# Expert rows of tiles 2 and 3 gathered as one 8 KB row of u and v, v weighted by a diagonal matrix on TensorE

## The reference, cut to what matters

```python
s = einsum('nhpd,hpkd->nhpk', q, sub_keys)               # scores against two sets of 128 sub-keys
s_top, i_top = top_k(s, 16)                              # 16 best of each half
best, sel = top_k((s_top[..., 0, :, None] + s_top[..., 1, None, :]).reshape(n, 8, 256), 16)
expert, gate = ..., softmax(best)                        # 8 x 16 = 128 experts a token
a = einsum('nd,ned->ne', x, take(u, expert))             # a dot of the token with each u row
act = gelu(a) * gate
out = einsum('ne,ned->nd', act, take(v, expert))         # weighted sum of the v rows
```

## Time and profile before

| | |
|---|---|
| median of 3 runs | 1908.88 us (1908.41 to 1910.58) |
| the profiled execution | 1910.62 us, its span 1908.6 us |
| TensorE busy | 1289.2 us (68%), mean granted clock 0.797 |
| VectorE busy | 1155.7 us (61%) |
| ScalarE busy | 372.3 us (20%) |
| POOL busy | 1095.1 us (57%), 1152 gathers |
| DMA | 725.45 MB, 380 GB/s over the span; 604.05 MB of it the gathers |

### The profile page before, as it was taken

How to read it: one execution, slowest core, us unless ns; L and a number is a source line. 1 busy time by engine, 2 the same in 40 slices (tenths; PEclk the granted TensorE clock), 3 DMA queues, 4 the chain that set the end, 5 groups by cost and what they waited for, 6 DMA issues and landing times.

```text
span 1908.6 us, 20116 instructions
## 1 busy us (share of the span) xinstructions
PE 1289.2 (68%) x6613; PEld 757.4 (40%) x6613; DVE 1155.7 (61%) x3160; ACT 372.3 (20%) x947; POOL 1095.1 (57%) x1192
## 2 busy tenths in 40 slices
PE   7898689998777787899977766664543433333344
PEld 5777565657454555555645422221220100000010
DVE  3117965566377657767755774568766667666430
ACT  3321133441021123234311110111101001000000
POOL 0002455446466656565656557666777777777764
PEclk9899888999888889999999877777765566555666
DMA  8567989899999999999999999999999999999997
GB/s 318 174 224 262 395 334 369 315 382 410 397 411 410 412 410 409 374 410 409 385 412 411 411 406 405 399 410 398 409 409 409 410 408 406 406 408 402 404 373 301
DMA packets 187013, 725.45 MB, mean 380 GB/s; under 512 B 21888, under 2 KB 23168, under 8 KB 174240
## 3 DMA queue, kind: packets, MB, share of 16 engines
q0 software_dynamic: 165888, 604.05, 80.4%
q1 hardware_dynamic: 18624, 117.55, 15.8%
q10 hardware_dynamic: 2400, 2.58, 0.4%
HBM read 719.16 MB, written 5.00 MB: 379 GB/s over the span
## 4 chain that ended last, share of the span: by engine, by line
PE 32%; DMA 31%; DVE 14%; POOL 13%; issue 8%; ACT 2%; SPq 0%; ACTq 0%; POOLq 0%; DVEq 0%
DMA v_ring<-in_peer_v,idx_v 15%; DMA u_ring<-in_peer_u,idx_u 14%; PE summed L1052 8%; POOL v_ring L740 6%; POOL u_ring L723 6%; DVE u_ring L1638 6%; PE bank L801 5%; PE bank L919 4%; PE bank L865 3%; PE bank L908 2%; PE bank L878 2%; PE bank L870 1%; PE bank L1022 1%; PE bank L997 1%; PE bank L1000 1%
## 5 line engine op out<-in xcount | busy, mean ns | idle before, releaser
L1638 DVE SCALAR_TENSOR_TENSOR u_ring<-u_ring,h_psum 128x1024 f32<-128x1024 f32 x576 | 689.9, 1215 | 276.4 <-DMA u_ring<-in_peer_u,idx_u 262.9
L1052 PE MATMUL summed<-v_ring,spread 128*32 128x512 f32 x2240 | 445.6, 857 | 496.8 <-DMA v_ring<-in_peer_v,idx_v 496.6
L740 POOL DMA_INDIRECT v_ring<-in_peer_v,idx_v x560 | 528.8, 944 | 411.5 <-PE summed L1052 216.1
L723 POOL DMA_INDIRECT u_ring<-in_peer_u,idx_u x576 | 543.4, 943 | 214.0 <-issue 116.5
L1052 PEld LDWEIGHTS summed<-v_ring,spread 128*32 128x32 f32 x2240 | 92.5, 138 | 766.0 <-issue 762.0
L801 PE MATMUL bank<-w_ring,hT 128*128 128x256 f32 (+1 forms) x720 | 184.3, 415 | 8.3 <-DVE shared L1525 3.8
L801 PEld LDWEIGHTS bank<-w_ring,hT 128*128 128x128 f32 (+1 forms) x720 | 139.7, 199 | 46.8 <-issue 16.4
L919 PE MATMUL bank<-hT,w_ring 128*128 128x128 f32 (+2 forms) x768 | 137.3, 336 | 1.6 <-issue 0.8
L919 PEld LDWEIGHTS bank<-hT,w_ring 128*128 128x128 f32 x768 | 121.0, 195 | 29.5 <-issue 22.6
L865 PE MATMUL bank<-hT,w_ring 128*128 128x192 f32 (+1 forms) x512 | 107.1, 364 | 1.5 <-DVE shared L1432 1.5
L713 POOL CAST idx_u<-experts 128x16 uint32<-128x16 f32 x36 | 7.8, 216 | 164.5 <-DVE gates L1628 164.3
(11 more groups left out here) (209 smaller groups left out, 1404.3 us busy)
## 6 DMA issues: line engine op xcount, KB each, us to landing
w_ring<-in_w_proj SPq DMA_DIRECT2D x27, 1024.0 KB, 8.4
w_ring<-in_w_pq SPq DMA_DIRECT2D x24, 1152.0 KB, 8.9
w_ring<-in_w_gate SPq DMA_DIRECT2D x24, 1024.0 KB, 8.1
w_ring<-in_w_z SPq DMA_DIRECT2D x12, 1024.0 KB, 7.6
w_ring<-in_w_out SPq DMA_DIRECT2D x12, 1024.0 KB, 9.6
u_ring<-in_peer_u,idx_u POOLq DMA_INDIRECT x576, 8.9
v_ring<-in_peer_v,idx_v POOLq DMA_INDIRECT x560, 8.8
qx<-in_x_prompt SPq DMA_DIRECT2D x8, 512.0 KB, 8.7
```

The lines of the kernel that those rows point to most:

```text
L723: nc.gpsimd.indirect_dma_start(u_ring[:, i % RING, :], None, peer_u, bass.IndirectOffsetOnAxis(idx_u[:, g % 2, j:j + 1], 0)).then_inc(u_la ...
L740: nc.gpsimd.indirect_dma_start(ring[:, slot, :], None, peer_v, bass.IndirectOffsetOnAxis(idx_v[:, n % 2, j:j + 1], 0)).then_inc(landed[slo ...
L1052: mm = nc.tensor.matmul(summed[half][low:low + 32, :], spread[:, P * i + 32 * c:P * i + 32 * c + 32], rows[:, 512 * half:512 * half + 512] ...
L1638: nc.vector.scalar_tensor_tensor(u, u, 1.0, h_psum[:], ALU.mult, ALU.mult, accum_out=dots_sb[:, g % 2, j:j + 1]).then_inc(u_free, 1)
```

## The change

For tiles 2 and 3 (ticks 320 to 575, 256 gathers) a third table `peer_uv` holds the u and the v row of an expert side by side, 8 KB. One gather (`gather_row`) brings both for each of 128 tokens, 1 MB, into a slot of 8 KB a partition: the two rings are one tensor now, and 8 such slots cover it. The v gathers of tiles 0, 1 and 4 still run until tick 353, in what was `v_ring`; so the first 36 rows use only the 4 slots over `u_ring`.

The dot of a row is as before (`dot_row`). Then ScalarE works row by row: `spread_gate` writes the identity times the gates (128x128) into one of 8 buffers `diag`, two rows ahead; `weigh_row` applies gelu to the one column of dots and multiplies the diagonal with it. TensorE multiplies this diagonal matrix with the v half of the row (`row_sums`, two matmuls of 128x128 by 512 columns), accumulating in two PSUM banks: for tile 2 in banks 2 and 3, which the front work hands over (from tick 320 on its jobs use banks 0 and 1 only), for tile 3 in `summed`. A slot is free once TensorE is done with the row (`row_summed`). The turning of experts and of weights (`places_t`, `spread`, `weigh`) goes away for these tiles, and so do the 34 ticks of v gathers behind the last u gather. The head items of part C stand at ticks 1, 3, 5 and 7 of a group instead of 1 to 4, and the norms 10, 11 and 12 eight ticks apart.

```diff
+SPLIT = GROUPS_C * GROUP
+MERGED = GATHERS - SPLIT
+UNITS = GROUPS_C // 2
+TICKS = GATHERS + 6
+DIAGS = 8
+AHEAD = 2
+FEW = 36
...
+def slot_of_row(m):
+    return m % 4 if m < FEW else (4 + m - FEW) % 8
...
+            n, off = divmod(j - 1, 2 if part == "C" else 1)
+            if 2 <= h < HEADS and off == 0 and 0 <= n < len(head_items(part, h)):
+                here.append(head_items(part, h)[n])
+                if n < 2:
...
+        tick = tick_of_sum(units_of_tile(t)[-1], 7) + 1 if k < 3 else gathers_of_tile(t)[-1] + 2
+        at(tick).insert(0, ("collect", t))
+        if k == 2:
+            for n in range(3):
+                at(tick + 1 + 8 * n).insert(0, ("norm", 10 + n))
+        if k > 2:
+            at(tick + 1).insert(0, ("norm", 10 + k))
...
+            b = len(jobs) % (BANKS if len(jobs) < len(split_jobs) else 2)
+            jobs[job] = (b, jobs_in_bank[b])
+            jobs_in_bank[b] += 1
...
+        ring = sb("ring", [P, 2 * RING, D])
+        u_ring, v_ring = ring[:, 0:RING, :], ring[:, RING:2 * RING, :]
+        uv_ring = ring[:].rearrange("p (s r) d -> p s (r d)", r=2)
+        diag = hT_all[:, 1024:1024 + P * DIAGS].rearrange("p (i n) -> p i n", n=P)
...
+            def gather_row(m):
+                g, j = divmod(SPLIT + m, GROUP)
+                if j == 0:
+                    copy_indices(g)
+                slot, former = slot_of_row(m), former_row(m)
+                if former is not None:
+                    pool.wait_ge(row_summed, former + 1)
+                elif slot < 4:
+                    pool.wait_ge(u_free, SPLIT - RING + 2 * slot + 2)
+                else:
+                    pool.wait_ge(v_free, SPLIT // 4 - 1 + (slot - 4) // 2)
+                nc.gpsimd.indirect_dma_start(
+                    uv_ring[:, slot, :], None, peer_uv,
+                    bass.IndirectOffsetOnAxis(idx_u[:, g % 2, j:j + 1], 0)).then_inc(row_landed[slot], 16)
...
+            for tick in range(GATHERS):
+                if tick < SPLIT:
                     gather_u(tick)
-                if tick >= LEAD:
+                if LEAD <= tick < SPLIT + LEAD:
                     gather_v(tick - LEAD)
+                if tick >= SPLIT:
+                    gather_row(tick - SPLIT)
...
+            def row_sums(m):
+                t = group_place((SPLIT + m) // GROUP)[0]
+                mine = [i - SPLIT for i in gathers_of_tile(t)]
+                if m == mine[0] and t == 2:
+                    for b in (2, 3):
+                        pe.wait_ge(bank_used[b], jobs_in_bank[b])
+                elif m == mine[0]:
+                    pe.wait_ge(collected, 3)
+                pe.wait_ge(diag_ready, m + 1)
+                for half in range(2):
+                    mm = nc.tensor.matmul((bank[2 + half] if t == 2 else summed[half])[:], diag[:, m % DIAGS, :],
+                                          uv_ring[:, slot_of_row(m), D + 512 * half:D + 512 * half + 512],
+                                          start=(m == mine[0]), stop=(m == mine[-1]))
+                mm.then_inc(row_summed, 1)
...
+                if SPLIT < tick <= GATHERS:
+                    row_sums(tick - SPLIT - 1)
...
+            def spread_gate(m):
+                g, j = divmod(SPLIT + m, GROUP)
+                if j == 0:
+                    act.wait_ge(selected, g + 1)
+                if m >= DIAGS:
+                    act.wait_ge(row_summed, m - DIAGS + 1)
+                nc.scalar.activation(diag[:, m % DIAGS, :], ident, ACT.Copy,
+                                     scale=gates[:, g % KEPT * GROUP + j:g % KEPT * GROUP + j + 1]).then_inc(gate_spread, 1)
+            def weigh_row(m):
+                g, j = divmod(SPLIT + m, GROUP)
+                d = dots_sb[:, g % 2, j:j + 1]
+                act.wait_ge(row_dotted, m + 1)
+                nc.scalar.activation(d, d, ACT.Gelu).then_inc(row_gelu, 1)
+                act.wait_ge(row_gelu, m + 1)
+                act.wait_ge(gate_spread, m + 1)
+                nc.scalar.activation(diag[:, m % DIAGS, :], diag[:, m % DIAGS, :], ACT.Copy, scale=d).then_inc(
+                    diag_ready, 1)
+                if m + AHEAD < MERGED:
+                    spread_gate(m + AHEAD)
...
+                if SPLIT <= tick < GATHERS:
+                    weigh_row(tick - SPLIT)
...
+                    if t in PART["C"]:
+                        dve.wait_ge(row_summed, gathers_of_tile(t)[-1] - SPLIT + 1)
...
+            def dot_row(m):
+                g, j = divmod(SPLIT + m, GROUP)
+                slot = slot_of_row(m)
+                dve.wait_ge(row_landed[slot], 16 * turn_of_row(m))
+                t = group_place(g)[0]
+                if SPLIT + m == gathers_of_tile(t)[0]:
+                    dve.wait_ge(h_turned, COLLECTED.index(t) + 1)
+                u = uv_ring[:, slot, 0:D]
+                nc.vector.scalar_tensor_tensor(u, u, 1.0, h_psum[:], ALU.mult, ALU.mult,
+                                               accum_out=dots_sb[:, g % 2, j:j + 1]).then_inc(row_dotted, 1)
...
+        "peer_uv": np.concatenate([np.asarray(peer_u)[0], np.asarray(peer_v)[0]], 1),
```

More of the change, by code:

```diff
@@ L120, in units_of_tile, with gathers_of_tile, former_row, turn_of_row @@
     return [n for n in range(UNITS) if tile_of_unit(n) == t]
-COLLECTED = TILE_ORDER
-assert list(COLLECTED) == sorted(range(TILES), key=lambda t: units_of_tile(t)[-1])
-QUADS = GATHERS // 4
-LAST_QUADS = QUADS - 6
-def place_of_v(i):
-    q, c = divmod(i, 4)
-    if q < LAST_QUADS or (q - LAST_QUADS) % 4 >= 2:
-        return "v", q % 2 * 4 + c
-    return "u", q % 2 * 4 + c
-def turn_of_v(i):
-    kind, slot = place_of_v(i)
-    return sum(place_of_v(m) == (kind, slot) for m in range(i % 4, i + 1, 4)) + (GATHERS // RING if kind == "u" else 0)
+def gathers_of_tile(t):
+    return [GROUP * g + j for g in range(GROUPS) if group_place(g)[0] == t for j in range(GROUP)]
+def slot_of_row(m):
+    return m % 4 if m < FEW else (4 + m - FEW) % 8
+def former_row(m):
+    return next((k for k in range(m - 1, -1, -1) if slot_of_row(k) == slot_of_row(m)), None)
+def turn_of_row(m):
+    return sum(slot_of_row(k) == slot_of_row(m) for k in range(m + 1))
+COLLECTED = TILE_ORDER
+assert list(COLLECTED) == sorted(range(TILES), key=lambda t: gathers_of_tile(t)[-1])
 def tick_of_sum(n, i):
@@ L337, in plan @@
                 selected_at[item[1]] = tick
-        if tick % UNIT == 20:
+        if tick % UNIT == 20 and tick < SPLIT:
             here.append(("places_t", tick // UNIT))
@@ L415, in layer @@
     jobs = {}
+    jobs_in_bank = [0] * BANKS
+    split_jobs = [job for item in before for job in jobs_of(item)]
+    split_jobs += [job for tick in range(SPLIT) for item in slots.get(divmod(tick, GROUP), []) for job in jobs_of(item)]
     for item in order:
         for job in jobs_of(item):
-            jobs[job] = len(jobs)
+            b = len(jobs) % (BANKS if len(jobs) < len(split_jobs) else 2)
+            jobs[job] = (b, jobs_in_bank[b])
+            jobs_in_bank[b] += 1
     pieces, last_job = {}, {}
@@ L585, in layer @@
         h_turned = sem("h_turned")
+        row_landed = [sem(f"row_landed{i}") for i in range(RING)]
+        row_dotted = sem("row_dotted")
+        row_gelu = sem("row_gelu")
+        gate_spread = sem("gate_spread")
+        diag_ready = sem("diag_ready")
+        row_summed = sem("row_summed")
         def bank_of(job):
-            return bank[jobs[job] % BANKS]
+            return bank[jobs[job][0]]
         def full(eng, job):
-            n = jobs[job]
-            eng.wait_ge(bank_full[n % BANKS], n // BANKS + 1)
+            b, turn = jobs[job]
+            eng.wait_ge(bank_full[b], turn + 1)
         def used(eng, job):
-            n = jobs[job]
-            eng.wait_ge(bank_used[n % BANKS], n // BANKS + 1)
+            b, turn = jobs[job]
+            eng.wait_ge(bank_used[b], turn + 1)
         def release(job):
-            return bank_used[jobs[job] % BANKS]
+            return bank_used[jobs[job][0]]
         def piece_ap(w):
@@ L1044, in expert_sums @@
                 strips = 4 if t < 4 else 2
-                places = [place_of_v(4 * q + c) for c in range(4)]
-                for c, (kind, slot) in enumerate(places):
-                    pe.wait_ge((v_landed if kind == "v" else u_landed)[slot], 16 * turn_of_v(4 * q + c))
+                for c in range(4):
+                    pe.wait_ge(v_landed[(4 * q + c) % RING], 16 * ((4 * q + c) // RING + 1))
                 for half in range(2):
@@ L1294, in _ @@
             for tick in range(TICKS):
-                if tick and tick % GROUP == 0 and tick <= GATHERS:
+                if tick and tick % GROUP == 0 and tick <= SPLIT:
                     gelu(tick // GROUP - 1)
+                if tick == SPLIT:
+                    for m in range(AHEAD):
+                        spread_gate(m)
+                if SPLIT <= tick < GATHERS:
+                    weigh_row(tick - SPLIT)
                 for item in slots.get(divmod(tick, GROUP), ()):
```

(6 more changed lines are left out.)

67 lines of the change are left out of this document (27 added, 40 removed).

## The result

Timed in 20 pairs, the changed kernel takes 1902.9 us (1898.7 to 1908.3) where the kernel before takes 1910.7 (1907.2 to 1917.9): the ratio is 0.9958, 95% interval 0.9946 to 0.9970. It is faster by 0.42%, 7.7 us by the medians. Forecast were 1899 us and 0.5%, range 1881 to 1927.

What follows compares the result with a forecast made beforehand. The DMA engines, full from tile 2's first dot on, were taken as the bound. 1908.6 - 22.2 (rate) - 7.7 (idle) + 19 (head groups) + 0.8 (tail) = 1898.5, forecast 1899 us, 0.5% faster, range 1881 to 1927.

Steps and rivals of the forecast that it cites:

- head groups: Groups 22 to 25 (ticks 354 to 415), heads still projected and scored: 45.5 us each against 39.7, taken as +19 us.
- Rate: Gathers of tiles 2 and 3: 8 KB rows at 422 GB/s, 2.482 us each, -22.2 us (0 to -27.8).
- The idle of before, -7.7: From tile 2's first dot to the last landing: 7.7 us of idle or half idle DMA, some 5 behind the last dot, go.
- The two parts follow each other: Groups 22 to 25: VectorE's 18.7 us, then TensorE's 25.1 and 1.7 at the seam, once the ring's slack is used up.
- Signs in the profile after: Later trace: 418 to 427 GB/s behind tick 416, head groups' DMA share under 0.95; first 34 ticks much over 128 us means wrong.
- Clock: TensorE in tiles 2 and 3: 74% busy, evenly, so 2.4 GHz throughout, against a granted 0.57 before.
- The weight loads in the open: TensorE's row products: by the skill's rule four exposed loads a row, an estimated 2.14 us; 1.83 was taken.
- POOL: Issuing gathers: 1.24 us each (0.94 busy) if 8 KB rows cost the same; no bound even at twice that.
- Tail: From the last landing to the end: about 12.3 us, +0.8 us against before.
- R1: Rival for the head groups: all is hidden, they stay at the DMA's pace, +19 not paid: 1880 us; chance 0.12.
- R2: Rival for the gathers: 8 KB rows run at 409 GB/s, no rate gained, +15: 1914 us; chance 0.14.
- R3: Rival on TensorE's price: 2.3 us a row and 4.8 a projection, +31: 1930 us; chance 0.32.

Runs made afterwards that it cites:

- the two gathers of 4 KB: Against the changed kernel, each expert row of tiles 2 and 3 fetched by two 4 KB gathers instead of one of 8 KB: 1916.3 us, 1.0019 of the kernel before.

## Why the prediction was right, point by point

The kernel got faster by what was forecast within 0.1%, and the mechanism was in the main the one named. That the sum came out so near is in part luck: the loss in the head groups was smaller than taken, and losses outside them, taken as none, made up for it. By its steps:

- **Rate.** 2.482 us a row taken; 421 GB/s give 2.49 (1.049 MB / 0.421). The bound by the weights' rows of 8 KB had been near. The term was -22.2 and is -20: 34 x 1.282 + 255 x 2.49 = 678.5 instead of 698.7. (Its bound of -27.8 was miscounted: 34 x 1.282 + 255 x 2.456 = 669.9, so -28.8.) The Trainium skill (DMA: Bandwidth & Descriptors, "Why small descriptors are slow") has about 3 cycles of overhead a packet, from which the prediction estimated 1.1%. The trace does not agree: 409 to 421 is 2.9%. That it comes from the row size is made likely, not shown, by the two gathers of 4 KB, which also doubled POOL's issues.
- **The idle of before, -7.7.** Its drain (4.84 us of POOL's wait) is gone, since the last dot waits for the last landing. I did not test it by itself.
- **Head groups.** +19 taken. From the first dot's end (1185.3) to the last landing (1894.47) are 709.2 us; less 678.5 and 10.2 of other transfers, 20.5 us were lost. They were in part elsewhere: rows 34 to 112 took 211.1 against 78 x 2.49 = 194.2, so 17, of which 3 are the 1.31 MB of other transfers that move there, and 14 are the loss; the first 34 rows 139.2 against 134.0 (5, and I had taken 0, with up to 10 left open); rows 112 to 255 4, of which 1 is other transfers. Group 22 took 50.3 us (its first row's dot starts at 1317.00), groups 23 to 25 took 45.3, 42.4 and 42.4, where 45.5 was worked out for each; the 36.7 of the group behind give 3 back. ScalarE and TensorE were each mis-sized, in opposite directions. The 128x128 product on ScalarE took 402 ns and not 267 (the nearest row had another source, PSUM instead of SBUF, and I had no row for the form itself); a pass of TensorE followed the other in 0.43 us, not 0.467, a row in 1.72 instead of 1.83.
- **The two parts follow each other.** Shown: taking TensorE's work away shortens these groups and the first 34 rows, adding some lengthens the head groups alone, and moving the selection away from the scores gives back 7 us.
- **Signs in the profile after.** The first 34 ticks took 139.2 us, where much over 128 was named as a sign of being wrong in kind: about 6 of the 11 us more are other transfers, which the 128 had left out, and 5 are TensorE's work. The DMA share in the head groups was to be under 0.95 and was 0.98; there the rate fell and the share did not.
- **Clock.** 2.4 GHz throughout was expected; the granted clock is 0.94 over the head groups and 1.00 in 1600 to 1700 us. It fell several times (in part around 1185, 1290, 1305 and 1590 us as well). The longest fall in the head groups is this one, at 1.2 GHz (columns as in the table of stretches). TensorE had stood for 1.92 us before the row at 1354.71; the gap of 4.4 us before the row at 1361.52, which took 3.78 us, came after the fall had begun:

```profile
1356.50:1369.00 12.50, 7.54 (x9) 2.68 (x9) 8.52 (x18) 9.21 (x21) 1.87 (x2) 0.50 1.00 404
```

- **The weight loads in the open.** The Trainium skill (TensorE: Matmul & The Clock Gate, "Part 3: Packing small matmuls") has weight loads overlap running matmuls only where the row group differs, from which the prediction estimated 2.14 us a row. The trace does not agree: the passes stood 0.43 us apart, 1.72 us a row.
- **POOL** 0.945 us for 1 MB: as taken.
- **Tail.** 12.3 us taken, 12.0 measured (1894.47 to 1906.5).

R1 (1880) fell with the head groups, R2 (1914) with the 421 GB/s. R3's condition arose only in short stretches, but the changed kernel stands near it: with a quarter more of TensorE's price a row (0.43 on 1.72 us) it was 0.5% slower than the kernel before. Along a straight line between the two runs, an estimate, the gain is gone at 0.2 us more a row (0.43 x 0.42 / 0.90).

## What to carry to other kernels

When two streams that freed their buffers separately are merged into one row, every engine that touches the row is in the path of every buffer: work it out for a whole period, with all that stands between in each queue, not by busy shares. An engine that waits for a result of another which itself waits for rows makes their work follow each other; moving such a consumer three places back gave 0.35%, nearly as much as the merge itself with its 0.42%. Compare traces from the point where the programs part: chance before it was as large as the effect.
